# First tile's mix taken into the last mixer head, with pieces moved between engines and across stage seams

## The chip, the cores and the metric

The kernel runs on one core of a Trainium2 chip, in float32. The metric is the device time of one execution in microseconds (us), the median of several runs. The names of the engines here: PE is TensorE, DVE is VectorE, ACT is ScalarE, POOL is GpSimd, and SP issues plain DMAs.

## The reference

One layer of a hybrid backbone, for 128 context tokens and 1024 latent tokens (nine tiles of 128 rows, the first of them the context), width 1024:

```python
h = rms_norm(x, g_norm1) * (1 + sc1) + sh1
mix = concat([bg * conv3(cg * xg), mlstm(q, k, v, gates) * sigmoid(og)]) @ w_out   # 4 heads, both directions
x = x + ga1 * mix
h2 = rms_norm(x, g_norm2) * (1 + sc2) + sh2
x = x + ga2 * peer(h2)
y = rms_norm(x, g_final)
# peer, per token and each of 8 heads: the 16 best of 128 * 128 experts,
# w = softmax(best) * gelu(h2 . u[expert]);  out = sum of w * v[expert]
```

The latent scans start from the context's state; the convolution runs per grid row of 64 tokens.

## The kernel before, in words

The program is a chain of four blocks with a barrier between each two of them. `modulation_stage` makes the six modulation vectors and the normed, transposed `hT`. `context_stage` does all of the context tile up to its chosen experts; its last part (eight rounds of top-k on DVE) is where PE also projects v, q and k of the first latent head (`project_first`). `mixer_stage` does the four latent heads one after the other. `peer_stage` does tile after tile the experts of the latent tiles: 1024 gathers of 1 MB each (one u and one v row per token), dots on DVE, sums on PE.

Inside a mixer head PE runs a fixed list of jobs, `BODY`, which alternate between two PSUM regions; a job may start when its region was evicted (`free`, the wait in `take`). The names: `ktok`, `vtok` turn k and v; `og`, `cg`, `xg`, `bg` and the next head's `q`, `k`, `v` are projections of 16 matmuls each; `s` is the score; `u0`, `u1` and `a0`, `a1` spread gate rows for the two directions; `kv`, `num` are the scan's products; `hT` turns the result. For direction d, DVE's `arguments` (L1196) takes `u` out of PSUM as eight tensor_scalars and frees its region, ACT takes the exponential (L1118), and DVE's `weights` makes `kw` (L1207), the masked `seen` (L1211) and its product with the scores (L1214).

Between these pieces DVE works on the context tile's own experts, the "picks": 256 gathered rows of 512 KB, 128 dots (L1178) and then 128 weighted additions (L1182). `BESIDE` says how many picks stand at each of nine places of each head; the call `beside(h, place)` runs them. POOL issues their gathers (L997) into a ring of eight rows, each after DVE has read the row eight before. What is left of the picks (21) is done at the start of `peer_stage` (L1690, gathers at L1423). Between the two stages stands the first latent tile's mix: PE multiplies its rows, which SP has stored to `scratch_cat` and loads again, with `w_out` (L1473); then DVE's `residual` and `modulate`, PE's transposes, the first query, scores and choice; and then the first 1 MB gathers (L1437) can be issued, of which the third waits for the last pick.

## Time and profile before

| | us |
|---|---|
| runs (median of 3) | 3586.84 (3585.72 to 3594.46) |
| the profiled execution | 3596.01, span 3594.3 |
| busy: PE, DVE, POOL, ACT | 3003.1, 2539.0, 1523.6, 911.1 |
| mean granted TensorE clock | 0.934 of full speed |
| HBM traffic | 366 GB/s over the span |

The shares over the whole span hide that the stages have different limits: from about 944 us on the DMA engines are busy at 1.00 of their time, before that they are not. The page's slices show it: the DMA line reads 8555787675 over the first ten slices and 9 or more after it.

### The profile page before, as it was taken

To read this page: it belongs to the slowest core of one execution; us is meant where nothing else is said; L and a number is where in the kernel's file an instruction comes from. 1 tells how busy PE (TensorE), PEld (TensorE's weight loads), DVE (VectorE), ACT (ScalarE), POOL (GpSimd) and SP (SyncE) were. 2 spreads that over 40 slices of the span, in tenths; PEclk is the share of its full clock that TensorE was granted. 3 is DMA by queue.
4 is the path that set the end of the run, shared out by engine and by line. 5 is a ranking of instruction groups with operands and counts; after the bars stand their busy time and mean duration, and the time that the engine had idled before them with its cause. 6 is when DMAs were issued, how large, how long until landed. Compare 5 with 4: busy or idle time off the path is not lost.

```text
span 3594.3 us, 33409 instructions
## 1 busy us (share of the span) xinstructions
PE 3003.1 (84%) x10068; PEld 1526.5 (42%) x10068; DVE 2539.0 (71%) x6056; ACT 911.1 (25%) x2291; POOL 1523.6 (42%) x1301
## 2 busy tenths in 40 slices
PE   6986979896488888898888888888888888888887
PEld 4753434443244434444443444344434434443443
DVE  3457777784766777777777767777777777677765
ACT  1211111111122323222233223223222232232222
POOL 0003565340444544454444444444444444444442
PEclk8987989897799999999999999999999999999999
DMA  8555787675999999999999999999999999999998
GB/s 354 178 157 191 244 306 276 226 285 197 364 416 413 407 420 419 408 408 417 408 408 416 416 412 409 413 418 411 415 406 413 395 419 415 411 401 420 420 412 339
DMA packets 227809, 1317.53 MB, mean 367 GB/s; under 512 B 24688, under 2 KB 44592, under 8 KB 95024
## 3 DMA queue, kind: packets, MB, share of 16 engines
q0 software_dynamic: 184320, 1208.04, 83.2%
q1 hardware_dynamic: 43312, 107.36, 8.1%
q8 instruction: 83, 1.36, 0.1%
q14 instruction: 94, 0.77, 0.1%
HBM read 1305.29 MB, written 10.01 MB: 366 GB/s over the span
## 4 chain that ended last, share of the span: by engine, by line
DVE 31%; PE 20%; DMA 15%; issue 3%; ACT 3%; DVEq 2%; POOL 1%; POOLq 0%
PE acc L1507 15%; DMA room<-in_uv,expert 15%; DVE room L1745 15%; PE mix L1473 3%; PE ps_q L1451 2%; DVE wt L1658 2%; ACT gelu L1564 2%; DVE work L1642 1%; DVE work L1638 1%; DVE picked L1645 1%; DVE ind L1606 1%; DVE ind L1599 1%; DVE pos L1626 1%; ACT diag L1570 1%; DVE work L1600 1%
## 5 line engine op out<-in xcount | busy, mean ns | idle before, releaser
L1507 PE MATMUL acc<-room,diag 128*128 128x512 f32 x4096 | 1947.2, 625 | 389.7 <-ACT diag L1570 389.5
L1437 POOL DMA_INDIRECT room<-in_uv,expert x1024 | 1232.3, 1203 | 1400.2 <-PE acc L1507 1198.2
L1745 DVE CUSTOM_DVE_ANT_0 room<-room,h 128x1024 f32<-128x1024 f32 x1024 | 1230.4, 1221 | 364.8 <-DMA room<-in_uv,expert 362.4
L1507 PEld LDWEIGHTS acc<-room,diag 128*128 128x128 f32 x4096 | 784.0, 199 | 1454.1 <-issue 1453.6
L1570 ACT ACTIVATE diag<-ident,wt 128x128 f32<-128x128 f32 x1024 | 377.4, 397 | 505.7 <-PE acc L1507 399.0
L1564 ACT ACTIVATE gelu<-dot 128x2 f32<-128x2 f32 x512 | 104.4, 204 | 1220.8 <-DVE dot L1745 1219.7
L1009 PE MATMUL region<-hT_then_w_out,w 128*128 128x512 f32 x800 | 368.6, 622 | 38.8 <-DVE seen L1196 32.5
L997 POOL DMA_INDIRECT room<-in_uv,cexpert x235 | 267.0, 1136 | 234.8 <-DVE acc L1182 123.0
L1658 DVE SCALAR_TENSOR_TENSOR wt<-gelu,rz,ex 128x2 f32<-128x2 f32 x512 | 113.6, 222 | 268.3 <-ACT gelu L1564 268.3
L1009 PEld LDWEIGHTS region<-hT_then_w_out,w 128*128 128x128 f32 x800 | 158.8, 201 | 240.4 <-issue 240.4
L1451 PEld LDWEIGHTS ps_q<-h2T,wq 128*128 128x128 f32 x2048 | 243.2, 195 | 40.4 <-issue 31.2
L1451 PE MATMUL ps_q<-h2T,wq 128*128 128x128 f32 x2048 | 243.8, 278 | 10.2 <-DMA wq<-in_wq 9.0
L1178 DVE CUSTOM_DVE_ANT_0 room<-room,ch 128x1024 f32<-128x1024 f32 x128 | 151.6, 1226 | 26.9 <-DMA room<-in_uv,cexpert 25.3
L1182 DVE SCALAR_TENSOR_TENSOR acc<-room,acc 128x1024 f32<-128x1024 f32 x107 | 137.8, 1288 | 9.7 <-issue 0.9
L1473 PE MATMUL mix<-hT_then_w_out,next_h 128*128 128x512 f32 x256 | 116.2, 599 | 8.5 <-DMA next_h<-scratch_cat 8.5
L1564 ACT ACT_TABLE_LOAD x79 | 101.4, 1283 | 1.4
L988 POOL MEMSET junk<- 128x1 f32 x2 | 0.1, 98 | 217.6 <-POOLq L357 217.6
L1745 DVE DVE_READ_ACCUMULATOR2_ANT dot<- 128x1 f32 x1024 | 83.9, 82 | 0.0
L1536 ACT ACT_TABLE_LOAD x64 | 82.1, 1283 | 1.1
L1473 PEld LDWEIGHTS mix<-hT_then_w_out,next_h 128*128 128x128 f32 x256 | 49.2, 193 | 70.5 <-issue 70.5
L1527 ACT COPY qs<-ps_q 128x256 f32<-128x256 f32 x64 | 23.8, 372 | 182.4 <-PE ps_q L1451 182.4
L1103 ACT ACTIVATE room<-region 128x1024 f32<-128x1024 f32 x24 | 24.4, 1017 | 135.3 <-PE region L1009 106.2
(301 smaller groups left out, 1997.4 us busy)
## 6 DMA issues: line engine op xcount, KB each, us to landing
w<-in_w_in SPq DMA_DIRECT2D x49, 512.0 KB, 5.1
room<-in_w_ada SPq DMA_DIRECT2D x12, 2048.0 KB, 17.3
room<-in_uv,expert POOLq DMA_INDIRECT x1024, 11.4
room<-in_wq SPq DMA_DIRECT2D x8, 1024.0 KB, 6.9
wq<-in_wq SPq DMA_DIRECT2D x1, 7168.0 KB, 29.3
xt<-in_x SPq DMA_DIRECT2D x9, 512.0 KB, 19.2
out_y<-x SPq DMA_DIRECT2D x9, 512.0 KB, 8.4
room<-in_w_out SPq DMA_DIRECT2D x2, 2048.0 KB, 12.0
```

The lines of the kernel that those rows point to most:

```text
L997: nc.gpsimd.indirect_dma_start(out=ring[k % RS], out_offset=None, in_=t["uv_rows"], in_offset=bass.IndirectOffsetOnAxis(ap=s["cexpert"][:, ...
L1009: last = nc.tensor.matmul(reg(name)[:, a:b], w[:, PROJ[name], k, :], hT[:, k, P + a:P + b], start=(k == 0), stop=(k == KC - 1))
L1178: nc.vector.tensor_tensor_reduce(out=row, in0=row, in1=s["ch2"][:], scale=1.0, scalar=0.0, op0=ALU.mult, op1=ALU.add, accum_out=dot[:, k:k ...
L1182: nc.vector.scalar_tensor_tensor(out=acc[:], in0=row, scalar=wt[:, k - PICKS:k - PICKS + 1], in1=acc[:], op0=ALU.mult, op1=ALU.add).then_i ...
L1437: nc.gpsimd.indirect_dma_start(out=uv[:, k % RING, :], out_offset=None, in_=t["uv"], in_offset=bass.IndirectOffsetOnAxis(ap=expert[:, h % ...
L1451: last = nc.tensor.matmul(ps_q[:, half, :], wq[:, k, (2 * c + half) * P:(2 * c + half + 1) * P], h2T[:, k, :], start=(k == 0), stop=(k == ...
L1473: last = nc.tensor.matmul(mix[:, a * BANK:(a + 1) * BANK], cat[:, k, :], wo[:, k, a * BANK:(a + 1) * BANK], start=(k == 0), stop=(k == KC ...
L1507: last = nc.tensor.matmul(acc[i % 2][:, a * BANK:(a + 1) * BANK], diag[:, k % DIAG, :], uv[:, k % RING, D + a * BANK:D + (a + 1) * BANK], ...
L1564: nc.scalar.activation(gelu[:, h % 2, ks], dot[:, h % 2, ks], ACT.Gelu).then_inc(gelued, 1)
L1570: nc.scalar.activation(diag[:, k % DIAG, :], ident[:], ACT.Copy, scale=wt[:, h % 2, k:k + 1]).then_inc(diagonal, 1)
L1658: nc.vector.scalar_tensor_tensor(out=wt[:, h % 2, ks], in0=gelu[:, h % 2, ks], scalar=rz[:, h % 2:h % 2 + 1], in1=ex[:, h % 2, ks], op0=AL ...
L1745: last = nc.vector.tensor_tensor_reduce(out=uv[:, k % RING, 0:D], in0=uv[:, k % RING, 0:D], in1=h2[:], scale=1.0, scalar=0.0, op0=ALU.mult ...
```

## The change

Eight edits that belong together:

- The first latent head's `og` and `cg` are projected and evicted at the end of `context_stage`, and left out of the mixer's first head.
- POOL gathers the first four picks at the end of `context_stage`, and the mixer's POOL list runs eight gathers ahead of its picks, into the peer stage (`begun`).
- `arguments` goes from DVE to ACT: eight Relu with the column as bias and scale -1, which free the region of `u`, then Exp with scale -1. The column is stored negated for that (the context's own tensor_scalar subtracts instead).
- `kw` goes from DVE to ACT: eight copies scaled by a column of `seen`.
- The two mask products of a head leave DVE: POOL writes `sT_back` and `sT`, each masked by an affine_select, behind a head's 22nd gather.
- `BESIDE`: 69 picks a head in place of 67 (38 in place of 34 in the last), 22 of them ahead of the head's first `weights`. 11 stay for the peer stage, 10 of them ahead of `residual`.
- The first tile's columns are also written to `cat0` on the chip, and PE multiplies them with `w_out` inside the last head: seven of eight column blocks ahead of `hT`, the last behind it. Its modulation vectors are loaded and combined there too.
- The peer stage starts without the mix, and loads the query weights ahead of the vectors; the third gather's wait stays, the seventh waits for the combined gain.

The diff, cut to its core:

```diff
-def left_out(h, name, region=None):
+ELSEWHERE = {(0, "og"), (0, "cg")} | {(HEADS - 1, name) for name in HANDED_ON}
...
 # context_stage
+                pool.wait_ge(state_out, 16 * 12)
+                pool.wait_ge(chosen, 1)
+                for k in range(cx["early"]):
+                    nc.gpsimd.indirect_dma_start(
+                        out=cx["ring"][k], out_offset=None, in_=t["uv_rows"],
...
+                project_first(3, OG)
+                project_first(4, CG)
...
+                act.wait_ge(q_done, 5)
+                act.wait_ge(first_done, 4)
+                nc.scalar.activation(og0, pp[1][:], ACT.Sigmoid).then_inc(first_taken, 1)
+                act.wait_ge(first_done, 5)
+                nc.scalar.copy(cg0, pp[0][:]).then_inc(first_taken, 1)
                 soften(PH - 1)
...
 # mixer_stage
-    BESIDE = ((16, 7, 7, 4, 4, 3, 7, 4, 15), (16, 7, 7, 4, 4, 3, 7, 13, 6), (16, 7, 7, 4, 4, 3, 7, 4, 15),
-              (16, 7, 7, 4))
+    BESIDE = ((22, 5, 7, 4, 4, 3, 7, 4, 13), (22, 5, 7, 4, 4, 3, 7, 7, 10), (22, 5, 7, 4, 4, 3, 7, 4, 13),
+              (22, 5, 7, 4))
+    MASK_AFTER = 22
...
+        cx["begun"] = min(PICKS + V_PICKS + RS, 2 * PICKS)
...
+                        if name == "bg" and h == HEADS - 1:
+                            sp.wait_ge(ready, 2 * HEADS)
+                            for vector, v in (("gate1", 2), ("gain", 4), ("shift", 3)):
+                                sp.dma_start(cx[vector], mod_vector(t, 1, v)).then_inc(vec0_in, 16)
+                            sp.wait_ge(jobs_done, job_done(h, "bg"))
+                            sp.dma_start(gfin, t["g_final"].partition_broadcast(P)).then_inc(wo_in[1], 16)
+                            for a in range(2):
+                                sp.dma_start(wo[:, :, a * BANK:(a + 1) * BANK],
...
-                for k in range(PICKS + V_PICKS):
+                starts = [sum(map(sum, BESIDE[:h])) for h in range(HEADS)]
+                for k in range(cx["early"], cx["begun"]):
+                    if k - MASK_AFTER in starts:
+                        wait_evicted(pool, starts.index(k - MASK_AFTER), "s")
+                        nc.gpsimd.affine_select(out=sT_back[:], in_=sT, compare_op=ALU.is_ge, fill=0.0, base=0,
+                                                pattern=[[0, NL], [-1, P]], channel_multiplier=1)
+                        pool.drain()
+                        nc.gpsimd.affine_select(out=sT, in_=sT, compare_op=ALU.is_ge, fill=0.0, base=0,
+                                                pattern=[[0, NL], [1, P]], channel_multiplier=-1).then_inc(masked, 1)
                     if k >= RS:
                         pool.wait_ge(c_read, k - RS + 1)
...
+                def mix_first(ks):
+                    for k in ks:
+                        for a in range(2):
+                            nc.tensor.matmul(mix0[:, a * BANK:(a + 1) * BANK], cat0[:, k, :],
+                                             wo[:, k, a * BANK:(a + 1) * BANK], start=(k == 0),
+                                             stop=(k == 2 * HEADS - 1))
...
+                    if h == HEADS - 1:
+                        wait_evicted(pe, h, "bg")
+                        wait_evicted(pe, h, "num1")
+                        for a in range(2):
+                            pe.wait_ge(wo_in[a], 16 + 16 * a)
+                        mix_first(range(2 * HEADS - 1))
                     pe.wait_ge(h_ready, h + 1)
...
                     def exps(d):
-                        wait_evicted(act, h, f"u{d}")
-                        nc.scalar.activation(seen[:], seen[:], ACT.Exp).then_inc(exped, 1)
+                        act.wait_ge(jobs_done, job_done(h, f"u{d}"))
+                        for c in range(NL):
+                            last = nc.scalar.activation(seen[:, c, :], tiles(f"u{d}")[:, c], ACT.Relu, scale=-1.0,
+                                                        bias=cols[:, d, 0, c + 1, h:h + 1])
+                        last.then_inc(free[region_of(f"u{d}")], 1)
+                        act.drain()
+                        nc.scalar.activation(seen[:], seen[:], ACT.Exp, scale=-1.0)
+                        act.drain()
+                        for c in range(NL):
+                            last = nc.scalar.activation(kw[:, c, :], ktok[:, c, :], ACT.Copy,
+                                                        scale=seen[:, c, end:end + 1])
+                        last.then_inc(weighted, 1)
                         evict(f"a{d}", qa, tiles(f"a{d}"))
...
                     def weights(d):
-                        dve.wait_ge(exped, h * 2 + (d + 1))
+                        if d == 0:
+                            dve.wait_ge(masked, h + 1)
+                        dve.wait_ge(weighted, h * 2 + (d + 1))
                         nc.vector.tensor_copy(dec[:], qa[:, :, end])
-                        nc.vector.tensor_tensor(kw, ktok, seen[:, :, end:end + 1].to_broadcast([P, NL, P]),
-                                                ALU.mult).then_inc(weighted, 1)
                         nc.vector.tensor_tensor(qa, qa, by_tile(qT[:]), ALU.mult)
-                        nc.vector.tensor_tensor(seen[:], seen[:],
-                                                masks[:, d, :].unsqueeze(1).to_broadcast([P, NL, P]), ALU.mult)
-                        nc.vector.tensor_tensor(seen[:], seen[:], sT, ALU.mult).then_inc(ready, 1)
+                        nc.vector.tensor_tensor(seen[:], seen[:], sT_back[:] if d else sT, ALU.mult).then_inc(ready, 1)
...
 # peer_stage
-    BESIDE_MIX, BESIDE_QUERY = 0, 0
+    BESIDE_MIX, BESIDE_QUERY = 10, 0
...
                 context(begun, begun + BESIDE_MIX)
-                dve.wait_ge(latent_in, 4 * 16)
-                nc.vector.scalar_tensor_tensor(out=gain[:], in0=gain[:], scalar=1.0, in1=g2, op0=ALU.add, op1=ALU.mult)
-                residual(0, gate1[:])
-                modulate(0, gain[:], shift[:])
+                residual(0, cx["gate1"])
+                modulate(0, cx["gain"], cx["shift"])
```

Where instructions stand now, at three places. The first is ACT in a head's first half (the second head, from the eviction of `s` to the division of direction 0). Before:

```order
L1103 ACTIVATE room<-region 128x1024 [waits jobs_done]
L1118 ACT_TABLE_LOAD
L1118 ACTIVATE seen<-seen 128x1024 [waits region_free0]
L1103 ACTIVATE room<-region 128x1024 [waits jobs_done] x2
L1125 ACTIVATE room<-region,den 128x128 [waits den_ready]
```

Now:

```order
L1163 ACTIVATE room<-banks 128x1024 [waits jobs_done]
L1180 ACTIVATE seen<-banks,cols 128x128 [waits jobs_done]
L1180 ACTIVATE seen<-banks,cols 128x128 x7
L1184 ACT_TABLE_LOAD
L1184 ACTIVATE seen<-seen 128x1024
L1188 ACTIVATE room<-room,seen 128x128 x8
L1163 ACTIVATE room<-banks 128x1024 [waits jobs_done] x2
```

ACT waits for PE's job and no longer for DVE's freed region; it has 16 small instructions more per direction.

The second is POOL's list from the mixer on. Before:

```order
L997 DMA room<-in_uv,cexpert 128x1024 x8
L997 DMA room<-in_uv,cexpert 128x1024 [waits c_read] x227
L945 UNCONDITIONAL_BRANCH
L1417 UNCONDITIONAL_BRANCH [waits barrier_Pool_Activation_PE_DVE_SP_gather]
L1419 IOTA iota 128x16
L1423 DMA room<-in_uv,room 128x1024 [waits c_read] x21
```

Now (four gathers of L414 stand before it in the context stage; the pair of L1030 and L1033 with 69 gathers behind it comes three times):

```order
L1038 DMA room<-in_uv,cexpert 128x1024 x4
L1038 DMA room<-in_uv,cexpert 128x1024 [waits c_read] x14
L1030 AFFINE_SELECT sT_back<-room 128x1024 [waits region_free1]
L1033 AFFINE_SELECT room<-room 128x1024
L1038 DMA room<-in_uv,cexpert 128x1024 [waits c_read] x69
```

Behind the wait for the scores' region stand all later gathers of POOL.

The third is PE from the end of the last head to the first transposes of the peer stage. Before:

```order
L1087 MATMUL region<-ident,room 128x128 [waits region_free0,h_ready]
L1087 MATMUL region<-ident,room 128x128 x7
L945 UNCONDITIONAL_BRANCH
L1442 UNCONDITIONAL_BRANCH [waits barrier_Pool_Activation_PE_DVE_SP_release]
L1473 MATMUL mix<-hT_then_w_out,next_h 128x512 [waits cat_in,wo_in0]
L1473 MATMUL mix<-hT_then_w_out,next_h 128x512 x3
```

Now:

```order
L1057 MATMUL banks<-hT_then_w_out,wg 128x512 [waits wo_in0,wo_in1,region_free1,region_free0]
L1057 MATMUL banks<-hT_then_w_out,wg 128x512 x13
L1143 MATMUL banks<-ident,room 128x128 [waits region_free0,h_ready]
L1143 MATMUL banks<-ident,room 128x128 x7
L1057 MATMUL banks<-hT_then_w_out,wg 128x512 [waits started]
L1057 MATMUL banks<-hT_then_w_out,wg 128x512
L974 UNCONDITIONAL_BRANCH
```

Fourteen of the mix's sixteen matmuls, and the wait for both halves of `w_out`, stand ahead of the transposes of the last head.

## Rows read from the trace of the kernel before

**Rows 1.** Busy time by stage: stretch, length, engines (x instructions), granted clock, DMA share, GB/s.

```profile
280.80:305.50 24.70, 0.00 (x1) 0.00 (x0) 20.93 (x90) 2.17 (x8) 0.03 (x1) 0.58 0.00 0
305.50:460.80 155.30, 127.65 (x377) 63.95 (x378) 110.33 (x197) 22.86 (x48) 93.95 (x79) 0.87 0.77 275
460.80:610.00 149.20, 128.98 (x376) 64.30 (x376) 110.57 (x192) 24.34 (x50) 86.22 (x69) 0.89 0.76 275
610.00:756.90 146.90, 126.81 (x377) 63.03 (x377) 116.27 (x128) 22.87 (x48) 62.73 (x67) 0.90 0.74 266
756.90:868.60 111.70, 87.83 (x280) 47.50 (x280) 73.82 (x94) 19.79 (x45) 24.38 (x27) 0.84 0.54 190
868.60:944.10 75.50, 30.42 (x108) 20.65 (x108) 42.88 (x64) 4.93 (x8) 21.68 (x24) 0.68 0.90 342
944.10:3594.30 2650.20, 2274.99 (x6612) 1093.05 (x6612) 1927.38 (x4901) 757.78 (x1968) 1230.46 (x1022) 0.96 1.00 410
```

**Rows 2.** Waits of PE in the mixer: who waited for whom, total, times, longest.

```profile
PE region L1009 <- DVE seen L1196: 32.5, 7, 10.6
...
PE region L1027 <- DVE mixed_rows L1294: 17.3, 3, 8.5
PE region L1045 <- ACT room L1125: 16.2, 4, 4.5
...
PE region L1009 <- ACT num L1125: 6.3, 1, 6.3
```

**Rows 3.** Groups of DVE in the mixer: count, busy, mean ns, idle before.

```profile
L1178 DVE CUSTOM_DVE_ANT_0 room<-room,ch 128x1024 f32<-128x1024 f32 x128 | 151.6, 1226 | 26.9 <-DMA room<-in_uv,cexpert 25.3
...
L1196 DVE TENSOR_SCALAR seen<-region,cols 128x128 f32<-128x128 f32 x64 | 17.2, 341 | 1.2 <-PE region L1045 0.9
...
L1211 DVE TENSOR_TENSOR seen<-seen,masks 128x1024 f32<-128x1024 f32 x8 | 9.7, 1218 | 0.0
```

**Rows 4.** A group of ACT in the mixer.

```profile
L1125 ACT ACTIVATE num<-region,den 128x128 f32<-128x128 f32 x32 | 8.7, 382 | 103.4 <-DVE den L1240 103.4
```

**Rows 5.** A group of POOL, whole run.

```profile
L406 POOL TENSOR_SCALAR_AFFINE_SELECT select<-select 4x512 f32<-4x512 f32 x1 | 0.6, 628 | 0.0
```

**Rows 6.** Timeline of POOL in the first head: start, length, idle time before.

```profile
349.67 1.98 POOL L997 DMA_INDIRECT room<-in_uv,cexpert  x1 [0.30 <-issue]
351.96 0.94 POOL L997 DMA_INDIRECT room<-in_uv,cexpert  x1 [0.30 <-issue]
```

**Rows 7.** Timeline of the context stage's end, PE and ACT.

```profile
262.16 13.90 PE L446 MATMUL ctx_pp<-hT_then_w_out,w 128*128 128x512 f32 x32
...
304.81 0.31 ACT L609 ACTIVATE cex<-ctx_best,ctx_neg_best 128x16 f32<-128x16 f32 x1 [9.01 <-DVE cexpert L832]
```

**Rows 8.** Timeline of PE in the third head: `cg`, and the next head's `k`.

```profile
634.20 16.66 PE L1009 MATMUL region<-hT_then_w_out,w 128*128 128x512 f32 x32 [2.58 <-DVE seen L1196]
...
685.57 16.57 PE L1009 MATMUL region<-hT_then_w_out,w 128*128 128x512 f32 x32 [5.46 <-DVE seen L1196]
```

**Rows 9.** Timeline from the last head's `bg` to the third 1 MB row.

```profile
847.86 1.23 DVE L1274 TENSOR_TENSOR mixed_rows<-region,y 128x1024 f32<-128x1024 f32 x1 [10.99 <-PE region L1009]
...
861.55 1.97 PE L1087 MATMUL region<-ident,room 128*128 128x128 f32 x8 [10.16 <-DVE room L1289]
...
872.04 15.50 PE L1473 MATMUL mix<-hT_then_w_out,next_h 128*128 128x512 f32 x32 [8.52 <-DMA next_h<-scratch_cat]
...
887.59 1.23 DVE L1665 TENSOR_TENSOR next_h<-mix,gate 128x1024 f32<-128x1024 f32 x1 [0.65 <-PE mix L1473]
...
914.94 28.91 DVE L1690 SCALAR_TENSOR_TENSOR acc<-room,acc 128x1024 f32<-128x1024 f32 x21
...
944.12 1.32 POOL L1437 DMA_INDIRECT room<-in_uv,expert  x1 [7.63 <-DVE acc L1690]
...
950.58 1.23 DVE L1745 CUSTOM_DVE_ANT_0 room<-room,h 128x1024 f32<-128x1024 f32 x1 [2.94 <-DMA room<-in_uv,expert]
```

**Rows 10.** The page's DMA issues: count, KB each, median us to landing.

```profile
hT_then_w_out<-in_w_out SPq DMA_DIRECT2D x2, 2048.0 KB, 12.5
```

135 lines of the change are left out of this document (78 added, 57 removed).

## The prediction

> **What bounds the kernel now.** I read the busy time by stage first [rows 1]. From 944.1 us on the DMA engines are busy at 1.00 and move 410 GB/s for 2650 us. That is 2.59 us for each of the 1024 rows of 1 MB; PE (2275 us) and DVE (1927 us) wait there. The change touches nothing in this stretch, so it can only move its beginning. Ahead of it no engine is full: the DMA share is 0.54 to 0.77 in the four heads, PE is busy 82 to 86% of the first three, DVE 71 to 79%. So the second view is the waits of PE in the mixer [rows 2]: 32.5 us in seven waits for DVE's `arguments`, which free the region of `u`; 17.3 us at three head ends for DVE's `mixed_rows`; 16.2 us in four waits for ACT's division; 6.3 us once for the second division. PE and DVE pass the lead back and forth there. Third, the end of the mixer and the seam behind it [rows 9]: from the block's start at 868.6 it takes 75.5 us until the third 1 MB gather is issued, and 28.9 us of that are picks.
>
> The sum is made against the profiled execution, 3596.0 us with a span of 3594.3. It lies 9.2 us above the median of the runs, 3586.8. I take the difference from the trace and apply it to the median.
>
> **The change part by part.**
>
> *End of the context stage.* PE is idle there for 24.7 us [rows 1]. One projection takes 13.9 us at the granted clock of that place [rows 7], two 27.8, so PE ends at about 308.6. Behind that ACT still has a copy, a table and its last exponential. This last one ran at 304.81 [rows 7]; I estimate 2.5 us for the three (0.3, the exponential alone, to 4), so it ends near 311. The block ends 6.3 us later (4 to 8). The four early gathers run under DVE's top-k rounds, where the DMA share is 0.00 [rows 1]: no cost.
>
> *First head.* PE loses two projections (27.8 us) and the longest wait, 10.6 us [rows 2], which stood before `cg`. But DVE must now finish 22 picks before its first `weights`, and their rows come at the rate of DMA. DVE loses, per head, two `arguments` of 17.2/8 = 2.15 us, two `kw` and two mask products of 1.22 us [rows 3]: 9.2 us. It gains two picks and two small writes of `cat0`, 3.3 us; net 5.9. The head cannot become shorter than DVE's work, 110.3 - 5.9 = 104, plus about 13 us of waits for gathered rows (26.9 us in two heads of dots [rows 3]): 118. It cannot stay longer than 155.3 less DVE's 5.9 and the 7.4 us that I find for the third head: 142. Behind the first `weights` the order k, outer, `bg`, numerators stays on PE, and DVE waits for it as now; so I take neither end but 132: -23 (-37 to -13).
>
> *Third head.* PE waited 2.58 us before `cg` and 5.46 us before `k` [rows 8], both for `arguments`. ACT now frees the region by itself: eight pieces of that shape take ACT 8.7/4 = 2.17 us [rows 4], against 2.15 on DVE, directly after PE wrote `u`, while PE writes `a`. I leave 0.6 us of the 8.0: -7.4. At the head's end PE's wait for DVE (17.3 us at three ends) becomes shorter, since DVE has 5.9 us less to do, PE itself 7.4: I take 3 us. Sum -10.3 (-16 to -5).
>
> *Second head.* The same waits, about 7.4, and the 6.3 us for `num`, since 7 picks and no longer 13 stand ahead of it. I give back 3 us: its 22 first dots follow on 13 others, and rows then come more slowly than dots run. Sum -10.6 (-18 to -3).
>
> *Masks.* POOL's nearest row is 0.63 us for 512 elements [rows 5], so 1.26 for 1024 and 2.5 for a pair. A gather's descriptors take POOL 0.94 or 1.98 us [rows 6], a factor 2.1; a pair then takes 5.3 us. Eight rows of the ring are filled before the pause and last DVE eight dots, 8 x 1.18 = 9.5 us (151.6/128 [rows 3]). So 2.5 to 5.3 us, and up to 4 of waiting for the scores, are hidden; I set 0, and at worst a few us in heads whose rows are late anyway, which the 3 us above hold. The GPSIMD Engine Reference of the Trainium skill (Key points) says that POOL shares its SBUF interfaces with VectorE and contends with DVE instructions of two SBUF inputs. The two lengths of [rows 6] fit that; a sum by this rule would take the 5.3, and the cover is still longer.
>
> *Last head.* SP loads `w_out` when `bg` is done, now behind the final gain. Before, `bg` was done at 847.9 and the transposes began at 861.55 [rows 9], 13.7 us later. A half of `w_out` lands 12.5 us after its issue [rows 10]; with 0.5 MB more ahead of it I take 15 for both. So PE begins the mix 1.3 us after the place where its transposes began. 14 of 16 matmuls take 14/16 of 15.5 us [rows 9], 13.6, and only then come the transposes (2.0 us before, 1.0 behind warm work). That is +13.9 on the way to the block's end; the earlier `u` and `kw` give back about 2. Sum +12 (+4, if `w_out` lands early and PE mixes before the transposes are ready, to +17).
>
> *Seam.* DVE began `residual` 19.0 us after the block's start, when vectors and mix had arrived; now 10 picks of 28.9/21 = 1.38 us stand ahead and nothing else: 14.0. -5.0. From `residual` to the end of the choice is 27.4 us as before. Then 21 picks (28.9 us) become one pick and the combined gain (1.4 + 1.2): -26.3. The loads of the query weights go first on SP's queue and have the picks' 14 us and more until they are needed. The first two rows no longer land under the picks; that costs up to a row, 2.6, I take 1. Sum -30.3 (-31 to -28).
>
> +6.3 - 23 - 10.3 - 10.6 + 12 - 30.3 = -55.9; 3586.8 - 55.9 = **3531 us**. With all ends against it about -25, with all in favour about -90; they will not fall together, so the case's own range is 3512 to 3552.
>
> **Rivals.**
>
> *The heads keep their length.* The gathers are what bounds a head: 69 rows in place of 67, POOL's pauses added, and DVE waits where PE waited. For it: 26.9 us of DVE's idle time are waits for rows. Against it: DMA is at 0.74 to 0.77 in those heads, and the third and fourth head's weighted additions wait for no DMA. Then 6.3 + 12 - 30.3 = -12: 3575. Chance 0.12.
>
> *ACT is the wrong engine for `u`.* If ACT took three times DVE's 2.15 us, each direction's weights would come 4.3 us later, on the path in six of eight places: 26 us given back, 3557. Against it: 2.17 us for eight pieces of this shape [rows 4]. Chance 0.07. The rule is in ScalarE: Activation LUTs of the Trainium skill (Rules for kernel authors): relu on VectorE, which is there up to about three times as fast in bf16; these tiles are f32 out of PSUM, and the rows show no such ratio.
>
> *The masks starve the ring (slower).* POOL issues in order; while it masks, no gather starts. Where the pause is longer than the 9.5 us of cover, each microsecond more is paid four times. From 24 us on (9.5 + 56/4) all is lost. At 15 us for a select, 34 us a pause, the loss would be 4 x 24.5 = 98 and the time 3629. Against it: this needs twelve times the 1.26 us that the nearest row gives. Chance 0.04.
>
> *More falls off.* The mix hides in front of the transposes (+4) and the heads come close to their bounds (-37, -16, -18): 6.3 - 37 - 34 + 4 - 30.3 = -91, 3496. Chance 0.10.
>
> **How the numbers follow.** The forecast has 0.67. Range: 3503 to 3566 holds it, the second rival and the half of the last that comes out less extreme; left out are the first (0.12), the slower one (0.04) and the other half (0.05). A measurement of this kernel can tell 0.3% from no change, about 11 us: the first rival lies at this edge, and I give half of it to each side. Faster 0.67 + 0.07 + 0.10 + 0.06 = 0.90, same 0.06, slower 0.04.
>
> **What would show it.** In the profile of the changed kernel: the mixer's block starts near 312; PE has no wait of more than 1 us for `seen` before a projection; the second head begins 17 us earlier than now, the fourth some 37; PE waits for `w_out` behind the last numerators, and the transposes of the last head stand behind 14 mix matmuls; POOL's selects take 1.2 to 2.7 us; the third 1 MB gather is issued about 45 us after the peer stage's start and near 888 us of the span; the rest still takes 2650 us at 410 GB/s. The forecast is wrong if heads two and three stay above 145 us, if the last head grows by more than 20 us, or if the stretch behind the third gather changes its length by more than 10 us.

## The result and the profile after

The changed kernel takes 3557.0 us (median of four, 3556.4 to 3561.7), the kernel before 3586.5 in the runs beside it: a ratio of 0.9915, 95% interval 0.990 to 0.993. That is 29.5 us less where 55.9 were forecast. The direction was right and the range (3503 to 3566) held. The forecast size was nearly twice what came, and 3557 lies outside the case's own range of 3512 to 3552. Of the experiments below, one run of e5 and one of e8 took some 20 us longer than the others, at a granted clock of 0.90 where those had 0.94, and their intervals are wide for it.

The busy time by stage of the changed kernel, cut like [rows 1]: end of the context stage, the four heads, the seam up to the third 1 MB gather, the rest. The columns are stretch, length, busy time of PE, PEld, DVE, ACT and POOL, granted clock, DMA share, GB/s.

```profile
280.50:311.20 30.70, 27.67 (x66) 12.01 (x65) 21.10 (x91) 6.97 (x12) 0.00 (x1) 1.00 0.00 1
311.20:450.10 138.90, 103.69 (x313) 55.78 (x313) 104.91 (x183) 27.51 (x76) 94.84 (x77) 0.83 0.83 293
450.10:590.50 140.40, 126.81 (x376) 62.84 (x377) 105.73 (x174) 33.50 (x82) 90.75 (x75) 0.93 0.84 307
590.50:729.90 139.40, 127.74 (x377) 63.32 (x378) 110.43 (x112) 32.01 (x80) 66.80 (x71) 0.92 0.78 286
729.90:856.80 126.90, 103.12 (x312) 53.52 (x312) 71.70 (x81) 28.93 (x77) 38.76 (x41) 0.86 0.65 234
856.80:904.50 47.70, 12.02 (x76) 11.30 (x76) 30.45 (x54) 4.93 (x8) 5.84 (x7) 0.62 0.77 294
904.50:3555.00 2650.50, 2273.36 (x6612) 1089.23 (x6612) 1928.47 (x4900) 756.42 (x1968) 1243.75 (x1022) 0.96 1.00 410
```

Against [rows 1] the first head fell from 155.3 to 138.9, the second from 149.2 to 140.4, the third from 146.9 to 139.4, the last grew from 111.7 to 126.9, the seam fell from 75.5 to 47.7. The rest, counted from the third gather, is as long as in that profile, 2650 us at 410 GB/s; a second profile of the kernel before shows below that this is partly chance. Together with the end of the context stage, which grew from 24.7 to 30.7, the differences come to 39 us, the difference of the two spans (39.3).

The waits of PE in the mixer, to be read against [rows 2] (who waited for whom, total, times, longest):

```profile
PE banks L1094 <- ACT room L1197: 20.3, 4, 6.1
PE banks L1115 <- DVE states L1282: 16.6, 1, 16.6
PE banks L1075 <- DVE mixed_rows L1362: 12.4, 3, 4.6
PE banks L1057 <- DMA hT_then_w_out<-in_w_out: 12.2, 1, 12.2
...
PE banks L1050 <- ACT seen L1180: 1.9, 3, 0.6
```

The 32.5 us for `seen` have become 1.9 us, for ACT. In their place stand two waits that were not there: 16.6 us for the first head's `states`, and 12.2 us for `w_out` in the last.

### The profile page after: what moved, and what is told of

It reads as the page before. It is cut to its first block, busy times and chain, and to the rows that moved or that the text cites. A ratio compares the mean times of both kernels' runs of the same rounds, so it can differ in the third digit from the quotient of the medians.

```text
span 3555.0 us, 33488 instructions
## 1 busy us (share of the span) xinstructions
PE 3000.2 (84%) x10068; PEld 1521.5 (43%) x10068; DVE 2509.5 (71%) x5985; ACT 946.5 (27%) x2420; POOL 1548.9 (44%) x1309
## 4 chain that ended last, share of the span: by engine, by line
DVE 31%; PE 17%; DMA 17%; issue 4%; ACT 4%; DVEq 2%; POOL 1%; POOLq 0%
DMA room<-in_uv,expert 16%; DVE room L1815 15%; PE banks L1575 6%; PE acc L1575 6%; PE banks L1544 3%; DVE wt L1726 2%; ACT gelu L1632 2%; PE banks L1523 2%; DVE work L1710 1%; DVE work L1706 1%; DVE picked L1713 1%; DVE ind L1674 1%; ACT diag L1638 1%; DVE ind L1667 1%; DVE work L1668 1%
## 5 line engine op out<-in xcount | busy, mean ns | idle before, releaser
L1575 PE MATMUL banks<-room,diag 128*128 128x512 f32 x2048 | 979.4, 627 | 184.1 <-ACT diag L1638 184.0
L1575 PE MATMUL acc<-room,diag 128*128 128x512 f32 x2048 | 966.6, 620 | 193.5 <-ACT diag L1638 193.1
L1575 PEld LDWEIGHTS banks<-room,diag 128*128 128x128 f32 x2048 | 392.8, 199 | 719.8 <-issue 719.5
L1575 PEld LDWEIGHTS acc<-room,diag 128*128 128x128 f32 x2048 | 387.6, 197 | 724.3 <-issue 724.1
L1050 PE MATMUL banks<-hT_then_w_out,w 128*128 128x512 f32 x736 | 335.0, 616 | 1.9 <-ACT seen L1180 1.9
L1523 PEld LDWEIGHTS banks<-h2T,wq 128*128 128x128 f32 x2048 | 240.6, 193 | 31.2 <-issue 31.2
L1523 PE MATMUL banks<-h2T,wq 128*128 128x128 f32 x2048 | 241.0, 276 | 1.2 <-ACT h2T L1614 1.2
L1050 PEld LDWEIGHTS banks<-hT_then_w_out,w 128*128 128x128 f32 x736 | 144.4, 199 | 184.8 <-issue 184.8
L1251 DVE CUSTOM_DVE_ANT_0 room<-room,ch 128x1024 f32<-128x1024 f32 x128 | 152.9, 1234 | 24.5 <-DMA room<-in_uv,cexpert 22.7
L1255 DVE SCALAR_TENSOR_TENSOR acc<-room,acc 128x1024 f32<-128x1024 f32 x117 | 150.8, 1288 | 17.2 <-DMA room<-in_uv,cexpert 7.5
L1544 PE MATMUL banks<-hT_then_w_out,next_h 128*128 128x512 f32 x224 | 100.7, 592 | 0.0
L1595 ACT COPY qs<-banks 128x256 f32<-128x256 f32 x64 | 23.8, 372 | 177.0 <-PE banks L1523 177.0
L414 POOL DMA_INDIRECT room<-in_uv,cexpert x4 | 4.0, 988 | 151.9 <-DVE cexpert L850 151.0
```

The source lines that it names most:

```text
L1050: last = nc.tensor.matmul(reg(name)[:, a:b], w[:, PROJ[name], k, :], hT[:, k, P + a:P + b], start=(k == 0), stop=(k == KC - 1))
L1251: nc.vector.tensor_tensor_reduce(out=row, in0=row, in1=s["ch2"][:], scale=1.0, scalar=0.0, op0=ALU.mult, op1=ALU.add, accum_out=dot[:, k:k ...
L1255: nc.vector.scalar_tensor_tensor(out=acc[:], in0=row, scalar=wt[:, k - PICKS:k - PICKS + 1], in1=acc[:], op0=ALU.mult, op1=ALU.add).then_i ...
L1523: last = nc.tensor.matmul(ps_q[:, half, :], wq[:, k, (2 * c + half) * P:(2 * c + half + 1) * P], h2T[:, k, :], start=(k == 0), stop=(k == ...
L1544: last = nc.tensor.matmul(mix[:, a * BANK:(a + 1) * BANK], cat[:, k, :], wo[:, k, a * BANK:(a + 1) * BANK], start=(k == 0), stop=(k == KC ...
L1575: last = nc.tensor.matmul(acc[i % 2][:, a * BANK:(a + 1) * BANK], diag[:, k % DIAG, :], uv[:, k % RING, D + a * BANK:D + (a + 1) * BANK], ...
```

## The experiments

Each kernel was timed beside the kernel before. For the stages I use the profiled execution of each: from the first transposes of a head to the next, from the peer stage's first load to its first 1 MB gather ("to first 1 MB gather"), and from there to the end ("rest"). `before_again` is the kernel before, profiled a second time.

| kernel | median us | ratio to before (95%) | first transposes at | heads | to first 1 MB gather | rest |
|---|---|---|---|---|---|---|
| before (profile of the rows) | 3586.5 | | 305.6 | 155.1 149.3 146.9 111.7 | 65.8 | 2660.0 |
| before_again | 3588.5 | 0.9995 (0.9985 to 1.0006) | 308.8 | 155.2 147.9 145.1 111.5 | 68.0 | 2651.7 |
| changed | 3557.0 | 0.9915 (0.990 to 0.993) | 311.7 | 138.4 140.4 139.3 126.9 | 44.2 | 2654.0 |
| e1_sem_mask | 3553.0 | 0.9902 (0.9885 to 0.9918) | 314.6 | 137.3 137.8 137.3 125.9 | 44.3 | 2652.9 |
| e2_turn_first | 3554.7 | 0.9911 (0.9895 to 0.9928) | 311.0 | 136.5 141.2 137.8 122.1 | 45.1 | 2652.8 |
| e3_own_projections | 3553.3 | 0.9906 (0.989 to 0.9923) | 306.5 | 140.7 141.0 138.9 127.1 | 44.5 | 2652.8 |
| e4_dve_arguments | 3602.2 | 1.0040 (1.0026 to 1.0055) | 311.8 | 148.7 151.3 153.0 136.3 | 44.4 | 2655.1 |
| e5_dve_masks | 3544.6 | 0.9889 (0.9852 to 0.9926) | 314.6 | 133.1 134.8 137.9 125.8 | 44.3 | 2653.4 |
| e6_no_early | 3563.2 | 0.9930 (0.9915 to 0.9946) | 313.3 | 143.0 141.6 138.5 125.9 | 44.2 | 2653.5 |
| e7_tail_picks | 3544.3 | 0.9869 (0.9853 to 0.9886) | 313.1 | 140.9 141.6 139.3 126.8 | 31.0 | 2650.1 |
| e8_first_head_12 | 3557.1 | 0.9920 (0.9894 to 0.9947) | 312.6 | 133.7 139.0 139.1 126.7 | 44.5 | 2653.3 |
| e9_old_order | 3570.2 | 0.9942 (0.9927 to 0.9957) | 314.5 | 138.8 142.5 144.0 133.3 | 44.7 | 2651.7 |
| best_1 | 3527.7 | 0.9825 (0.9811 to 0.9838) | 313.5 | 134.2 136.5 139.0 122.1 | 31.0 | 2651.1 |
| best_2 | 3524.1 | 0.9819 (0.9806 to 0.9833) | 305.9 | 136.9 138.0 137.1 121.4 | 31.3 | 2651.8 |

The same code differs by 2 to 4 us in a head from one profile to another (first head 138.4, 136.5 and 140.9 in the changed kernel, e2 and e7, whose edits lie behind it), so smaller differences of one head are not read. Heads one to three of these three come to 418.2, 415.5 and 421.8 us together. The kernels were also timed on different occasions, and the kernel before itself then took 3586.5 (changed), 3588.5 (e1 to e4), 3591.6 (e5, e7, e8; in before_again 3588.5 on the same occasion) and 3590.4 us (e6, e9, best_1, best_2). So a difference of a few us between two medians, or between two ratios whose intervals overlap, shows nothing by itself; for e1, e2, e3, e6 and e8 the waits and lengths in the profiles have to speak. "Rival" in an expectation is the explanation that stands against theory A.

**The kernel before once more.**

> The kernel before once more, for its profile. If the profile that the prediction's rows come from was a long one by chance, this one has a span of 3580 to 3588, and the stages tell where the 8 us lie: in the heads (their lengths then differ by a few us from 155.3, 149.2, 146.9, 111.7) or in the gather-bound rest (2642 and not 2650 us). If instead the times outside a profile are shorter, the span is 3594 again.

Its span is 3588.2, and the 8 us lie in the rest: 2651.7 us from the first 1 MB gather, not 2660.0. All kernels after the change have 2650 to 2655 there. So the profile that the prediction's rows come from was long by chance in a stretch that the change does not touch. In before_again, POOL issues the first three 1 MB rows (L1437) like this (start, length, idle time before):

```profile
936.46 0.93 POOL L1437 DMA_INDIRECT room<-in_uv,expert  x1 [0.30 <-issue]
937.70 0.94 POOL L1437 DMA_INDIRECT room<-in_uv,expert  x1 [0.30 <-issue]
946.27 1.33 POOL L1437 DMA_INDIRECT room<-in_uv,expert  x1 [7.63 <-DVE acc L1690]
```

And those of the changed kernel:

```profile
901.02 1.68 POOL L1509 DMA_INDIRECT room<-in_uv,expert  x1 [38.79 <-DVE expert L1715]
903.00 1.18 POOL L1509 DMA_INDIRECT room<-in_uv,expert  x1 [0.30 <-issue]
904.49 0.94 POOL L1509 DMA_INDIRECT room<-in_uv,expert  x1 [0.30 <-issue]
```

Before, two rows were under way 8.6 to 9.8 us ahead of the third, to which I had counted; now the three start within 3.5 us. Counted to the first, the seam fell by 21.5 us (65.8 to 44.2) or, by the second profile, 23.8 (68.0 to 44.2). The second profile also sets the length of the rest right: counted from the third gather it is 2642.0 us there, 2650.2 in the profile of the rows and 2650.5 in the changed kernel.

**The masks: the drain between the selects.** In the changed kernel POOL's two selects of the second head stand far apart:

```profile
474.58 1.40 POOL L1030 TENSOR_SCALAR_AFFINE_SELECT sT_back<-room 128x1024 f32<-128x1024 f32 x1
484.37 1.09 POOL L1033 TENSOR_SCALAR_AFFINE_SELECT room<-room 128x1024 f32<-128x1024 f32 x1 [8.38 <-issue]
```

The selects are as short as forecast; but between them POOL does nothing for 8.4 us (27.0 in four heads), and no gather starts.

```diff
-                                                pattern=[[0, NL], [-1, P]], channel_multiplier=1)
-                        pool.drain()
+                                                pattern=[[0, NL], [-1, P]], channel_multiplier=1).then_inc(back_masked, 1)
+                        pool.wait_ge(back_masked, starts.index(k - MASK_AFTER) + 1)
```

> Between POOL's two mask selects the drain is replaced by a wait on the first select's own semaphore. Theory A (the drain also waits for gathers whose descriptors are still being worked off, and this pause is what heads one to three lack): the idle time between the two selects falls from 5.0 to 8.4 us to under 1 us, the first head from 138.4 to about 134 us, heads two and three by 1 to 3 us each, the whole by 4 to 10 us against the changed kernel (about 3550). Theory B (the ring covers the pause as forecast, the heads are held by the pace of the rows and by PE): the pause may shrink, but the time stays within 2 us of 3557. Theory C (the select's own completion takes that long): the idle time between the selects stays at 5 to 8 us.

The same place of e1:

```profile
475.46 1.10 POOL L1031 TENSOR_SCALAR_AFFINE_SELECT sT_back<-room 128x1024 f32<-128x1024 f32 x1
476.63 1.97 POOL L1034 TENSOR_SCALAR_AFFINE_SELECT room<-room 128x1024 f32<-128x1024 f32 x1
478.76 1.73 POOL L1039 DMA_INDIRECT room<-in_uv,cexpert  x1 [0.16 <-issue]
```

The idle time is gone (0.07 us in all four heads), so it was the drain and not the select. DVE's waits in the mixer, in the changed kernel, show what the drain did to it: waits of the dots for rows, of the weighted additions for rows, and for the masks.

```profile
DVE room L1251 <- DMA room<-in_uv,cexpert: 22.7, 23, 4.0
DVE acc L1255 <- DMA room<-in_uv,cexpert: 7.5, 9, 2.0
DVE dec L1271 <- POOL room L1033: 4.5, 3, 2.7
```

In e1 the second and the third are gone, and the first is shorter:

```profile
DVE room L1252 <- DMA room<-in_uv,cexpert: 15.9, 22, 3.7
```

That the drain is paid in rows is shown: e2, e3, e6, e7 and e8, which keep it, have 6.8 to 7.2 us of the second wait and 4.0 to 5.5 of the third, e1, e5 and e9 have neither. (e4 keeps the drain and has neither too; DVE is held there by its own arguments, as its experiment shows.) What it costs in time is less certain. The four heads together are 6.8 us shorter (545.1 to 538.3), about as much as the same code scatters, and the median 4.0, with overlapping intervals. The sum fits theory A at its lower end; the first head, which theory A saw at 134, takes 137.3. How a pause reaches DVE, in the first head of the changed kernel (POOL's second select and next gather, then DVE's next row):

```profile
345.01 1.59 POOL L1033 TENSOR_SCALAR_AFFINE_SELECT room<-room 128x1024 f32<-128x1024 f32 x1 [5.02 <-issue]
346.75 0.94 POOL L1038 DMA_INDIRECT room<-in_uv,cexpert  x1 [0.16 <-issue]
```

```profile
352.48 1.23 DVE L1251 CUSTOM_DVE_ANT_0 room<-room,ch 128x1024 f32<-128x1024 f32 x1 [3.23 <-DMA room<-in_uv,cexpert]
```

The first select begins at 338.57, with 22 rows issued and DVE in its 17th dot. The five rows left last until 345.66; the next is issued at 346.75, and DVE can read it at 352.48, 5.7 us later.

**The masks on DVE again.**

```diff
-                        nc.vector.tensor_tensor(seen[:], seen[:], sT_back[:] if d else sT, ALU.mult).then_inc(ready, 1)
+                        nc.vector.tensor_tensor(seen[:], seen[:],
+                                                masks[:, d, :].unsqueeze(1).to_broadcast([P, NL, P]), ALU.mult)
+                        dve.drain()
+                        nc.vector.tensor_tensor(seen[:], seen[:], sT, ALU.mult).then_inc(ready, 1)
```

POOL's two selects, `sT_back` and `masked` go.

> The masks go back from POOL to DVE (a product with the mask before the product with the scores), all else as changed, the 22 picks too. Theory A (DVE is loaded enough in the heads that its own 2.44 us per head count, more than the pauses of 8 to 12 us at POOL): time up by 2 to 10 us against the changed kernel. Rival (POOL's pauses cost the heads more than DVE's two products): the waits of DVE for rows behind the 22nd pick go, and the time falls by 2 to 6 us, as much as the semaphore in place of the drain gave.

12.4 us less, twice the upper end of the rival's 2 to 6; three of e5's four runs lie more than 10 us below every run of the changed kernel. By stages (the four heads of e5):

```profile
314.55:447.66 133.11, 103.90 (x313) 55.68 (x313) 106.18 (x185) 27.52 (x76) 89.06 (x70) 0.83 0.86 307
447.66:582.46 134.80, 127.05 (x377) 62.95 (x377) 107.26 (x176) 33.50 (x82) 88.43 (x73) 0.93 0.88 318
582.46:720.38 137.92, 127.60 (x377) 63.76 (x377) 112.68 (x114) 32.01 (x80) 64.67 (x69) 0.93 0.81 291
720.38:846.18 125.80, 101.89 (x312) 52.86 (x312) 74.10 (x83) 28.93 (x77) 35.55 (x38) 0.86 0.66 234
```

DVE is busy 1.3 to 2.4 us longer per head, and yet the first two heads are 5.3 and 5.6 us shorter: DMA moves 307 and 318 GB/s there, not 293 and 307. Why a pause of POOL is time taken from rows can be read in the first head of the changed kernel: the 18 gathers ahead of the first select start 1.49 us apart on average, with no wait for DVE between them, and DVE's dot takes 1.23. In e5 the waits for the masks and of the additions for rows are gone, and those of the dots fell from 22.7 us to 12.9:

```profile
DVE room L1244 <- DMA room<-in_uv,cexpert: 12.9, 15, 4.2
```

**The first head: two projections more or fewer.** `og` and `cg` of the first head go back into it, their evictions too.

```diff
-ELSEWHERE = {(0, "og"), (0, "cg")} | {(HEADS - 1, name) for name in HANDED_ON}
+ELSEWHERE = {(HEADS - 1, name) for name in HANDED_ON}
...
-                project_first(3, OG)
-                project_first(4, CG)
```

> og and cg of the first head go back from the context stage into the first head. Theory A (their place in the context stage is worth the PE work that they take out of a PE-bound head): the context stage ends 6 us earlier, the first head takes 27.8 us more, less the 16.6 us in which PE now waits there for DVE's states, so 150 us; the time rises by 4 to 8 us. Rival (the first head is held by DVE and its gathered rows, so PE's 27.8 us have room in it): the first head grows by under 5 us and the time falls by 1 to 6 us.

The rival holds: with 27.8 us of PE work more the first head is 2.3 us longer, no more than the scatter, and the mixer starts 5.2 us earlier. The median is 3.7 us lower, with overlapping intervals. PE's first numerators in the changed kernel, and then in e3:

```profile
362.53 0.77 PE L1115 MATMUL banks<-vtok,seen 128*128 128x129 f32 x2 [16.62 <-DVE states L1282]
```

```profile
349.99 13.90 PE L1042 MATMUL banks<-hT_then_w_out,w 128*128 128x512 f32 x32
363.72 0.39 PE L1106 MATMUL banks<-vtok,seen 128*128 128x129 f32 x2
```

They begin 51 us after the head's start in the one (362.53 - 311.65), 57 in the other, without a wait. What PE lost in the changed kernel it waited for.

**The first head: rows ahead of the first weights.** Masks behind the 12th row there, and 12 picks ahead.

```diff
-    BESIDE = ((22, 5, 7, 4, 4, 3, 7, 4, 13), ...
-    MASK_AFTER = 22
+    BESIDE = ((12, 5, 7, 4, 4, 9, 9, 4, 15), ...
+    MASK_AFTER = (12, 22, 22, 22)
```

> In the first head alone the masks come behind the 12th row and 12 picks, not 22, stand ahead of DVE's first weights; the ten others stand beside its second chain and bg. Theory A (the first head is held by the 22 rows ahead of the first weights, which the gathers deliver one per 1.3 us or slower): the first numerators begin 8 us earlier or more (354 and not 362.5), and the first head takes 130 to 135 us in place of 138.4. Rival (it is DVE's whole work, or the whole number of rows, that fills the head): the numerators come earlier, but the head keeps 137 us or more, since DVE or its rows are late at its end.

The numerators come 38.0 us after the head's start (350.6 - 312.6), 12.9 earlier, with 3.7 us of wait in place of 16.6, and the head takes 133.7, as theory A had it. But PE waits 12.1 us for the mixed rows at the head's end (3.5 in the changed kernel), so two thirds of the gain are given back there. PE's first numerators and the second head's first transposes in e8:

```profile
350.60 0.77 PE L1116 MATMUL banks<-vtok,seen 128*128 128x129 f32 x2 [3.70 <-DVE states L1283]
446.27 1.94 PE L1076 MATMUL banks<-ident,kT 128*128 128x128 f32 x8 [12.09 <-DVE mixed_rows L1363]
```

The times do not tell e8 from the changed kernel.

**The early gathers.**

```diff
-            cx = {"ring": ..., "slots": 8, "early": 4, ...
+            cx = {"ring": ..., "slots": 8, "early": 0, ...
```

> The four gathers at the end of the context stage are left to the first head; all else as changed. Theory A (the first head's 22 picks run at the pace of its gathers, so four rows in hand are worth four issues of POOL): the first pick begins 6 us later or more (319 and not 312.4), the first head takes 142 to 146 us in place of 138.4, the time rises by 3 to 7 us. Rival (the head's rows are late at other places anyway): under 2 us.

DVE's first rows then:

```profile
313.92 0.21 DVE L1233 COPY room<-cexpert 128x128 uint32<-128x128 uint32 x1
322.52 1.23 DVE L1251 CUSTOM_DVE_ANT_0 room<-room,ch 128x1024 f32<-128x1024 f32 x1 [8.38 <-DMA room<-in_uv,cexpert]
```

The first head takes 143.0, as theory A had it. The median is 6.2 us more, but the intervals overlap, and the kernel before beside it was 3.9 us longer too. DVE's first 8.4 us are a wait for the first row; with four rows in hand there is one wait of 4.0, for the fifth.

**ACT's part.** Arguments and weighted keys back on DVE.

```diff
+                    def arguments(d):
+                        dve.wait_ge(jobs_done, job_done(h, f"u{d}"))
+                        for c in range(NL):
+                            last = nc.vector.tensor_scalar(seen[:, c, :], tiles(f"u{d}")[:, c],
+                                                           cols[:, d, 0, c + 1, h:h + 1], 0.0, ALU.subtract, ALU.min)
+                        last.then_inc(free[region_of(f"u{d}")], 1)
...
+                    arguments(0)
                     weights(0)
```

> The arguments of the exponential and the weighted keys go back from ACT to DVE, all else as changed. Theory A (ACT's freeing of u's region is what took the 32.5 us of PE's waits for seen away, as forecast): these waits come back, 2 to 5 us in six of eight places, DVE has 27 us more to do in the mixer, and the time rises by 15 to 30 us, to about 3580. Rival (the gain of the heads comes from the masks and the order of the picks, not from ACT): the time rises by under 6 us.

45.2 us more, beyond both ranges. PE's waits in e4:

```profile
PE banks L1051 <- DVE seen L1258: 45.7, 6, 13.3
PE banks L1104 <- DVE room L1270: 31.8, 2, 28.5
```

The waits for `seen` are back, and longer than the 32.5 of [rows 2]. The longest wait, 28.5 us, is new: in the first head PE waits for the weighted keys, which DVE makes behind its 22 dots and the arguments. That the 22 picks (16 before) ahead of `arguments` make the waits longer is argued from their place; no run has the old order without ACT's part. The changed kernel without ACT's part is slower than the kernel before (1.004), so the other edits need it.

**The order of the picks alone.** Masks on DVE and ACT as changed; of the six picks two go behind the first weights, four behind `bg` or to the head's end (in the last head ahead of its first division). The totals stay.

```diff
-    BESIDE = ((22, 5, 7, 4, 4, 3, 7, 4, 13), (22, 5, 7, 4, 4, 3, 7, 7, 10), (22, 5, 7, 4, 4, 3, 7, 4, 13),
-              (22, 5, 7, 4))
+    BESIDE = ((16, 7, 7, 4, 4, 3, 7, 4, 17), (16, 7, 7, 4, 4, 3, 7, 11, 10), (16, 7, 7, 4, 4, 3, 7, 4, 17),
+              (16, 7, 7, 8))
```

> Masks on DVE, and the picks in the order of before (16 and not 22 ahead of the first weights, the six moved behind it), with the same number in each head. To be compared with the kernel that has only its masks on DVE (heads of 133.1, 134.8, 137.9 and 125.8 us). Theory A (with ACT freeing u's region, six picks fewer ahead of the first weights let the numerators begin earlier): PE's wait of 13.3 us for the first head's states shrinks by 5 us or more, and the first head to 127 to 130 us; the others stay within 2 us. Rival (rows are what the head waits for, and picks at its end delay the mixed rows): the first numerators come earlier, but PE's waits at the heads' ends grow by as much; each of the first three heads is equal or up to 5 us longer.

PE's wait for the first head's states falls from 13.3 to 8.0, as theory A had it. But the heads are 5.7 to 7.7 us longer than those of e5, and the median is 25.6 us higher; the rival holds, above its 5. The wait has moved to the ends of the first three:

```profile
PE banks L1068 <- DVE mixed_rows L1356: 28.7, 3, 11.7
```

In e5 it is 10.7 us, in as many waits. The run moved four of the six picks to late places of the head, so it shows that this order is worse, not that every order with 16 picks ahead would be.

**The last head: transposes ahead of the mix.**

```diff
                     project_next("v")
+                    pe.wait_ge(h_ready, h + 1)
+                    take("hT")
+                    for c in range(NL):
+                        last = nc.tensor.transpose(tiles("hT")[:, c], hsum[:, c, :], ident[:])
+                    last.then_inc(jobs_done, 1)
                     if h == HEADS - 1:
                         wait_evicted(pe, h, "bg")
```

> In the last head the eight transposes stand ahead of the mix instead of behind 14/16 of it. Theory A (the last head grows because the transposes, the last mixed rows and their store hang behind the mix): the transposes run at 834 to 836 us, inside the wait for w_out; the mix begins at 836 as now; the block ends when the mix does, near 852.5 instead of 856.8; the time falls by 4 us (3 to 5). Rival (the end is set by the mix alone, or the transposes delay the mix by their own 2 us): 0 to 2 us less.

The end of the last head in the changed kernel, on PE:

```profile
835.99 14.64 PE L1057 MATMUL banks<-hT_then_w_out,wg 128*128 128x512 f32 x28 [12.16 <-DMA hT_then_w_out<-in_w_out]
850.47 1.04 PE L1143 MATMUL banks<-ident,room 128*128 128x128 f32 x8
851.95 1.98 PE L1057 MATMUL banks<-hT_then_w_out,wg 128*128 128x512 f32 x4 [0.44 <-DVE wg L1356]
```

And in e2:

```profile
830.41 1.97 PE L1137 MATMUL banks<-ident,room 128*128 128x128 f32 x8 [10.16 <-DVE room L1348]
832.20 16.17 PE L1057 MATMUL banks<-hT_then_w_out,wg 128*128 128x512 f32 x32
```

The transposes fit into the wait for `w_out`, and the mix ends at 848.4, right ahead of the block's end (848.6). In the changed kernel the mix ended at 853.9, and the block at 856.8, with the store of the last mixed rows. The head is 4.8 us shorter, as theory A had it; the executions scatter (3548.3 to 3559.8) and don't show it by themselves. best_1 has the same last head, 122.1.

**The seam: eight picks into DVE's wait for bg.**

```diff
-              (22, 5, 7, 4))
+              (22, 5, 7, 4, 0, 0, 8))
...
-    BESIDE_MIX, BESIDE_QUERY = 10, 0
+    BESIDE_MIX, BESIDE_QUERY = 3, 0
```

> Eight picks more in the last head, between DVE's second chain and bg, where DVE waits 11.0 us for PE; two or three picks are left ahead of the residual behind the block's end, in place of ten. Theory A (the seam is as long as DVE's ten picks make it): the block ends within 1 us of 856.8; the residual begins 8 to 10 us earlier, near 864.5, the third 1 MB gather is issued near 895.5, and the time falls by 8 to 10 us. Rival (the loads behind the block's end, the next x, the query weights and the gains, bound the seam, or the eight rows come late and hold bg's eviction and with it the mix): the seam shrinks by under 4 us or the block ends 3 us later or more, and the time falls by 0 to 4 us.

DVE in e7, the eight picks in the last head:

```profile
814.36 2.67 DVE L1255 SCALAR_TENSOR_TENSOR acc<-room,acc 128x1024 f32<-128x1024 f32 x2
817.47 8.20 DVE L1255 SCALAR_TENSOR_TENSOR acc<-room,acc 128x1024 f32<-128x1024 f32 x6 [0.45 <-issue]
825.83 0.29 DVE L1332 TENSOR_TENSOR wg<-banks,y 128x128 f32<-128x128 f32 x1 [0.16 <-issue]
```

They fill the wait to 0.2 us. The last head stays at 126.8, the seam to the first gather falls from 44.2 to 31.0, the median by 12.7: theory A, and above its 8 to 10. That is more than the picks' own time, for in the changed kernel the ninth and tenth pick waited for their rows too:

```profile
868.80 1.29 DVE L1759 SCALAR_TENSOR_TENSOR acc<-room,acc 128x1024 f32<-128x1024 f32 x1 [0.87 <-DMA room<-in_uv,room]
872.56 1.29 DVE L1759 SCALAR_TENSOR_TENSOR acc<-room,acc 128x1024 f32<-128x1024 f32 x1 [2.47 <-DMA room<-in_uv,room]
```

**Put together.** best_1 is e5, e2 and e7; best_2 undoes the two early projections as well.

> Three edits on the changed kernel together: masks on DVE, transposes ahead of the mix in the last head, eight picks more in the last head. If they add up: heads near 133, 135, 138 and 121 us, 31 us from the block's end to the first 1 MB gather, and 12 + 4.5 + 13 = 29.5 us less than the changed kernel, 3527. If the last head's picks collide with the transposes (both end near 834 us) or the seam is bound by its loads once the block ends earlier: 3532 to 3538.

> The three edits together, and og and cg of the first head back in the first head. If the first head is held by its gathered rows here too: the context stage ends 5.5 us earlier, the first head takes 2 to 3 us more, and the time falls by 3 us against the three edits alone, 3524. If the masks' pause was what gave room to the two projections: the first head grows by 8 us or more, and the time rises by 2 to 4 us, 3530.

3527.7 and 3524.1: the parts add up. The 3.6 us between the two have the forecast sign and size (the first head is 2.7 us longer, the mixer starts 7.6 earlier), but the runs of the two overlap. best_2 takes 0.9819 of the kernel before, 66 us less than the 3590.4 measured beside it, and 33 less than the change as made.

## Why the prediction was right in direction, and where its size came from

The working by terms, against the two profiles of before (the second is before_again). The forecast of the seam was counted to the third 1 MB gather, the measured values to the first:

| term | forecast | profile of the rows | second profile |
|---|---|---|---|
| context end | +6.3 | +6.0 | +2.9 |
| first head | -23 | -16.7 | -16.8 |
| second head | -10.6 | -8.8 | -7.4 |
| third head | -10.3 | -7.5 | -5.8 |
| last head | +12 | +15.3 | +15.5 |
| seam, to the first 1 MB gather | -30.3 | -21.5 | -23.8 |
| from there to the end | 0 | -6.0 | +2.2 |
| sum | -55.9 | -39.3 | -33.2 |

**What was right.** The mixer's block begins at 311.2 (forecast near 312); over all profiles the first transposes begin at 313.1 in the ten kernels with the two projections in the context stage and at 306.7 in the four without (means), 6.4 us apart. The waits for `seen` are gone; the longest left is 0.6 us. That ACT is the place for the arguments and the weighted keys together is shown by e4. The rival that had Relu on ACT three times as slow fell: eight pieces take 2.18 us (321.36 in the first head), against 2.15 on DVE. ScalarE: Activation LUTs of the Trainium skill (Rules for kernel authors) prefers VectorE for relu; for these f32 tiles out of PSUM the trace shows no difference, and where the work stands decides. `w_out` arrived 15.3 us after its first issue, forecast 15. Every head's term came within its own bounds. Of the things that should show it, these came out smaller or later: the second head begins 10.7 us earlier (17 forecast), the fourth 27.0 (37), and the third gather is issued at 904.5 (888).

**What was luck.** The case's own range missed; the wide one holds 3557 since I stretched it for the rival with ACT as the wrong engine, which gives just this number and whose mechanism e4 and the 2.18 us refute. And none of the three signs of a wrong forecast came, but the third only because the profile of the rows was a long one: behind the third gather it has 2650.2 us, the changed kernel 2650.5. Against the second profile's 2642.0 that stretch grew by 8.5, close to the 10 that I had named, because its first two rows no longer land ahead of it.

**The step that failed most: the seam was counted to the third gather.** I let the first two "cost up to a row, 2.6, I take 1". Before, the first was under way 9.8 us ahead of the third, and the stream had its first two rows while DVE finished the picks; now it is 3.5 ahead. By this lead they cost 6.3 and not 1. Counted to the third, as I did, the seam fell by 27.8 (30.1 by the second profile), near the 30.3; the 2.5 that are missing by the profile of the rows are in `residual`, which began 17.2 us after the block's start and not 14.0, since its ninth and tenth pick waited for their rows. The gain that reaches the end is that of the first gather, 21.5 to 23.8: this rests on the second profile, from whose first gather the rest takes 2651.7 us, as after the change; its 3590.0 us lie in the middle of the runs of the kernel before. So 6.5 to 8.8 us of the forecast were never there. How much of them the rest gives back can't be told to better than the 5 us by which it scatters after the change (2650.1 to 2655.1).

**The first head's 132.** I chose a value between DVE's work with its waits for rows (118) and a PE bound (142). What held the head is what I had only named, "their rows come at the rate of DMA". PE's lost projections became a wait of 16.6 us (e3), and what shortens the head is rows: four early ones are worth 4.6 us of it (e6), POOL's pauses 5.3 (e5), each to be read with the scatter of 2 to 4. Ahead of the first select it is POOL's pace more than DMA's that sets the rows' (a gather every 1.49 us without a wait). By the second profile the head fell by 16.8 where 23 were forecast.

**The masks at 0.** The selects take 1.1 to 1.6 us each, a pair 2.2 to 3.0, at or below the lower end of the 2.5 to 5.3. What I did not price is the drain between them: 5.0 to 8.4 us of POOL, so a pause of 8 to 11 us. And the cover of eight dots, 9.5 us, did not hold: five rows were ahead and not eight, and a cover has to last until the next row has landed, 5.7 us behind its issue, not only until POOL goes on. In the four heads the masks cost 13.5 us by these profiles (545.1 to 531.6 in e5), of which the drain alone is 6.8 (e1); both carry the scatter of some 6 us that the same code has. The rival with starving masks had the right mechanism and too high a threshold; it was paid out of the gain, not beyond it. It can also hold the missing gain in heads two and three: with the masks on DVE the first three heads come to 405.8 us, forecast 407.4. Single heads are off by more, 133.1, 134.8 and 137.9 for 132.2, 138.6 and 136.6, so the agreement of the sums is partly luck.

One effect that the GPSIMD Engine Reference of the Trainium skill (Key points) lets one expect also shows: beside POOL's first select DVE's dot takes 1.96 us instead of 1.23. In e1 two dots take 1.97 and 2.10 there. Over all fourteen profiles 17 dots took longer than 1.3 us, each beside a select, and none in the six kernels whose POOL has no selects. The two lengths of a gather's descriptors [rows 6], which I had laid to the same cause, are not explained by it: in the changed kernel one takes 1.97 us at 313.59 and one 0.97 at 326.09, both beside running dots.

```profile
337.81 1.23 DVE L1251 CUSTOM_DVE_ANT_0 room<-room,ch 128x1024 f32<-128x1024 f32 x1
...
339.10 1.96 DVE L1251 CUSTOM_DVE_ANT_0 room<-room,ch 128x1024 f32<-128x1024 f32 x1
```

**The last head's +12.** The mix ahead of the transposes was costed at 13.9 for PE. Behind the transposes hang the last mixed rows and their store as well, which then end the block: +15.3, and 4.8 of it disappear when the transposes go first (e2).

**The baseline.** I took differences from one profile and applied them to the median. That profile had its extra 8 us in the gather-bound rest, which the terms leave out, so this step did the sum no harm; it only hid that the stretch behind the third gather grew. The second profile's 33.2 and the medians' 29.5 differ by no more than single executions do (3585.7 to 3594.5 of the kernel before).

What stays open: whether, and why, masks on DVE beat masks on POOL without a drain by 6.7 us in the heads (538.3 to 531.6), which is within the scatter. The pause of 2.4 to 3.6 us and DVE's slower dots are seen, their sum is not, and no run takes them apart. What the drain waits for is open too; that it ends with gathers still at work was a theory that no run tests.

## What to carry to other kernels

Where one engine issues all gathers in its order, each thing put between them is paid in rows as far as the rows in hand do not last until the next one has landed. Here a drain at that place cost 5.0 to 8.4 us of POOL, a semaphore on the one instruction that was meant 0.07. Work taken from an engine gives time only as far as the next thing in that stage is ready: before moving it, ask what its neighbour would then wait for. And count a stream's gain from its first transfer to the last, not from a later one that happens to be the one that waits.

## What the runs showed that was not expected

POOL's drain between the selects, behind indirect gathers, holds POOL for 5.0 to 8.4 us in the changed kernel and 4.0 to 8.4 over the seven kernels that have it; a wait on the select's semaphore at the same place leaves 0.07 us idle. And the same head of the same code differs by 2 to 4 us between executions, the gather-bound rest by up to 8.
